# The masked score chunks of block two's window attention: a matmul with a constant, or memsets on VectorE

## The chip, the cores and the metric

One Trainium2 chip, one NeuronCore of it. The metric is the device time of the whole program in microseconds (us). Engines are called PE (TensorE's matmuls), PEld (its weight loads, which overlap the matmuls), DVE (VectorE), ACT (ScalarE), POOL (GpSimd) and SP (SyncE, which issues the DMAs). Each engine works its own instructions in order; between engines, and between dependent instructions of one engine, there are only semaphores.

## The reference, cut to what matters

Two transformer blocks over 512 tokens of width 1024, all in fp32. The change touches only the attention of the second one. Tokens lie in chunks of 64; a query sees the keys of its own chunk, whole, and of the two chunks before it:

```
qc = q.reshape(B, nc, CHUNK, ATT_KV_HEADS, ATT_GROUP, HEAD_DIM)      # CHUNK = 64, 2 kv heads, 8 heads in a group
kb = concatenate([kc[:, j:j + nc] for j in range(WINDOW_CHUNKS + 1)], axis=2)   # 3 chunks of keys
s = einsum('bnqhgd,bnkhd->bhgnqk', qc, kb) * HEAD_DIM ** -0.5
s = where(key_chunk >= 0, s, -1e30)
m = maximum(max(s), sink)
p = exp(s - m)
denom = sum(p) + exp(sink - m)
o = einsum('bhgnqk,bnkhd->bnqhgd', p / denom, vb)
```

## The kernel before, in words

Precision is kept by splitting operands into two float32r parts (`_hi`, `_lo`). A projection's weights come by DMA into `stage`, ACT rounds them to `w_hi`, DVE subtracts to get `w_lo`, and PE makes three products of each piece (hi with hi, hi with lo, lo with hi).

The window attention is a software pipeline of 32 pieces in 35 steps (`WIN_STEPS`, a lag of 3). A piece is one block of 128 queries (`b = p // 8`) and two heads that share a bank of PSUM, one in each half of 256 columns. For `b > 0` a head has 256 keys, two blocks of 128, of which each half of the query block masks one chunk: queries 64 to 127 don't see the first 64 keys, and queries 0 to 63 don't see the last 64. For `b = 0` there is only the query block's own 128 keys, and only the second of these masks. The order is written out by hand and every engine's loop runs over the same `p`:

- PE, step p (L2315 to L2361): waits until ACT has read the scores of piece p-2 (`ps_s` has two buffers); the mask product (L2324), which writes the constant -1e30 or 0 over the outer chunks by a product of the identity with `window_r`; four score products (L2332, L2334), which add to it; then for piece q = p-3 the transposes of the divided weights (L2348), 5 or 6 products of 512 columns of the next projection (`stream`, L1956), and the products with the values into `ps_o` (L2358). The last ones wait for ACT's copy of the transposed weights (`win_pt_made`), and in every second step also for `a_gated`.
- DVE, iteration p (L1742 to L1787): in every second one two gate products that read `ps_o` (L1753, 64 partitions each, they set `a_gated`); the row maximum of the scores (L1762); its minimum with the sink (L1765); the sink's difference (L1768); for piece p-1 the denominator (L1776), its reciprocal (L1777) and the division of the second head's weights (L1779); and, in some iterations, a bank of the streamed projection (L1698), its gate (L1705) or half a `w_lo` (L1177).
- ACT, iteration p (L1029 to L1067): the copy of piece p-3's transposed weights (L1036, L1038 for `b = 0`), which waits for the transposes; the two exponentials of piece p (L1049), which wait for DVE's L1765; the sink's exponential (L1055); the division of the first head's weights of piece p-1 (L1061); and in some iterations a tanh (L1010) or half a `w_hi` (L662).

`link` gives a DVE instruction an increment of DVE's own semaphore and `after` waits for it: DVE's instructions do not see each other's results otherwise. Behind the attention PE goes on with the projections of `u2` (L2362), in the same order.

Of the kernel before, what the change touches and what calls it, by code (L numbers as in the profile page):

```python
# [33 lines left out]
P = 128  # L34
# [6 lines left out]
NEG = -1e30  # L41
# [12 lines left out]
CHUNK = 64  # L54
# [52 lines left out]
def window_head(i, e):  # L107

    return 4 * (i // 2) + i % 2 + 2 * e
# [81 lines left out]
def build(nc, A):  # L191
    with ExitStack() as ctx:
# [6 lines left out]
        def keep(name, shape, dt=F32):  # L199
            return ctx.enter_context(nc.sbuf_tensor(name, shape, dt))  # L200
# [13 lines left out]
        ident_r = keep("ident_r", [P, P], F32R)  # L214
        causal_r = keep("causal_r", [P, P], F32R)
        window_r = keep("window_r", [P, 2, 2 * P], F32R)
# [66 lines left out]
        ps_s = ctx.enter_context(nc.psum_tensor("ps_s", [P, 2, S], F32))  # L283
# [866 lines left out]
        def _(dve):  # L1150
            V = nc.vector
            chain = [0]

            def link(ins):

                chain[0] += 1
                ins.then_inc(dve_chain, 1)
                return chain[0]

            def after(n):  # L1160
                dve.wait_ge(dve_chain, n)
# [261 lines left out]
            for p in range(MLA_STEPS + 3):  # L1423
                if p < NP:
                    n = P * (p % 4 + 1)
                    b = p % 4
# [5 lines left out]
                if 1 <= p <= NP:  # L1432
                    q = p - 1
                    n = P * (q % 4 + 1)
                    b = q % 4
# [12 lines left out]
                for u, m in MLA_STREAM.banks.get(p, ()):  # L1448
                    n = 2 * (u - U0["dk"]) + m
# [36 lines left out]
            for p in range(DIFF_STEPS + 1):  # L1486
# [7 lines left out]
                if p < NP:  # L1494
                    n = P * (p % 4 + 1)
                    for e in range(2):
                        b = 2 * (p % 4) + e
# [5 lines left out]
                if 1 <= p <= NP:  # L1503

                    q = p - 1
                    n = P * (q % 4 + 1)
                    b, c = q % 4, q % 8
# [7 lines left out]
                    if b == 3:  # L1515
                        c = 4 * (q // 4 % 2)
# [185 lines left out]
            def z_bank(m, n):  # L1702

                dve.wait_ge(z_tanh, n + 1)
                V.scalar_tensor_tensor(out=gu[:, n, :], in0=tmp[:, m, :], scalar=1.0, in1=gu[:, n, :], op0=ALU.add,  # L1705
                                       op1=ALU.mult).then_inc(z_gated, 1)
# [35 lines left out]
            for p in range(WIN_STEPS + 2):  # L1742
                if p > LAG and (p - LAG) % 2 == 0 and p - LAG <= NP:

                    pair = (p - LAG) // 2 - 1
                    b, c0 = pair // 4, 2 * (pair % 4)
                    dve.wait_ge(win_pv_done, 2 * pair + 2)
                    if pair == 0:
                        dve.wait_ge(za_made, KD)
                    for odd in range(2):  # L1750
                        rr = slice(odd * AD, odd * AD + AD)
                        g = gz[rr, c0:c0 + 2, b * P:b * P + P]
                        V.tensor_tensor(g, ps_o[rr, 256 * odd:256 * odd + 256].rearrange("p (c n) -> p c n", c=2), g,  # L1753
                                        ALU.mult).then_inc(a_gated, 1)
                if p < NP:
                    b, i = p // 8, p % 8
                    h = window_head(i, 0)
                    j = 16 * (b % 2) + h
                    j0 = 0 if b else P
                    dve.wait_ge(win_s_full, p + 1)  # L1760
                    mx = nmax[:, 2 * (p % 4):2 * (p % 4) + 2]
                    after(link(V.tensor_reduce(mx, ps_s[:, p % 2, :].rearrange("p (e n) -> p e n", e=2)[:, :, j0:256],  # L1762
                                               AX.X, ALU.max, negate=True)))

                    V.tensor_tensor(nm2[:, j:j + 3:2], mx, nsinkb[:, h:h + 3:2], ALU.min).then_inc(win_max_made, 1)  # L1765
                    c = 2 * (p % 4)
                    dve.wait_ge(win_max_made, p + 1)
                    V.tensor_tensor(dsink[:, c:c + 2], sinkb[:, h:h + 3:2], nm2[:, j:j + 3:2], ALU.add  # L1768
                                    ).then_inc(sink_diff, 1)
                if 1 <= p <= NP:  # L1770
                    q = p - 1
                    b, i = q // 8, q % 8
                    j0, c = 0 if b else P, 2 * (q % 4)
                    j = 16 * (b % 2) + window_head(i, 0)
                    dve.wait_ge(sink_exp, q + 1)
                    after(link(V.tensor_tensor(den2[:, c:c + 2], rs2[:, j:j + 3:2], esink[:, c:c + 2], ALU.add)))  # L1776
                    V.reciprocal(rden2[:, c:c + 2], den2[:, c:c + 2]).then_inc(rden_made, 1)  # L1777
                    dve.wait_ge(rden_made, q + 1)
                    V.tensor_scalar(prob2[:, q % 4, 256 + j0:512], prob2[:, q % 4, 256 + j0:512], rden2[:, c + 1:c + 2],  # L1779
                                    None, ALU.mult).then_inc(win_p_ready, 1)  # L1780
                for u, m in WIN_STREAM.banks.get(p - 1, ()):
                    z_bank(m, 2 * (u - U0["zs"]) + m)
                for u, m in WIN_STREAM.banks.get(p, ()):
                    normed(gu[:, 2 * (u - U0["zs"]) + m, :], u, m)
                for h in range(2):
                    for u in WIN_STREAM.started(p - 3 - h):
                        lo_half(u + 1, h)  # L1787

            for i in range(4):
# [5 lines left out]
                for m in range(2):  # L1795
                    c = 2 * i + m
# [8 lines left out]
            for i in range(4):  # L1805
                u = U0["vs"] + i
                lo(u + 1)
                for t in range(TT if i % 2 else 0):
                    n = 4 * (i // 2) + t
# [29 lines left out]
            for i in range(4):  # L1839
                u = U0["att"] + i  # L1840
                lo(u + 1)
                for m in range(2):
                    c = 2 * i + m
# [19 lines left out]
            for i in range(4):  # L1863
                u = U0["sgo"] + i
                lo(u + 1)
                for m in range(2):
                    c = 2 * i + m
# [46 lines left out]
        def _(pe):  # L1914
            T = nc.tensor
# [195 lines left out]
            for p in range(MLA_STEPS):  # L2111
                if p < NP:
                    h, t = p // 4, p % 4
                    n = P * (t + 1)
# [39 lines left out]
            for p in range(DIFF_STEPS):  # L2154
                if p < NP:
                    h, t = p // 4, p % 4
                    n = P * (t + 1)
                    for e in range(2):
# [5 lines left out]
                        for k in (kd_hi, kd_lo):  # L2164
                            T.matmul(ps_s[:, e, 0:n], qd[:, 2 * h + e, t * P:(t + 1) * P], k[:, 2 * h + e, 0:n],  # L2165
                                     start=(k is kd_hi), stop=False)
# [148 lines left out]
            for p in range(WIN_STEPS):  # L2315
                if p < NP:
                    b, i = p // 8, p % 8
                    if p >= 2:
                        pe.wait_ge(win_exp_made, 2 * (p - 1))
                    j0 = 0 if b else P  # L2320
                    k0 = (b - 1) * P if b else 0

                    ends = slice(0, 4, 3) if b else slice(3, 4)
                    T.matmul(ps_s[:, p % 2, :].rearrange("p (e c n) -> p e c n", e=2, c=4)[:, :, ends, :],  # L2324
                             ident_r[:, :], window_r[:, :, :].rearrange("p e (c n) -> p e c n", c=4)[:, :, ends, :],
                             start=True, stop=False, skip_group_check=True)


                    for e in range(2):
                        h = window_head(i, e)  # L2330
                        out = ps_s[:, p % 2, e * 256 + j0:e * 256 + 256]
                        T.matmul(out, q_split[:, h, b * P:(b + 1) * P], k_hi[:, i // 4, k0:(b + 1) * P],  # L2332
                                 start=False, stop=False, skip_group_check=True)
                        ins = T.matmul(out, q_split[:, h, b * P:(b + 1) * P], k_lo[:, i // 4, k0:(b + 1) * P],  # L2334
                                       start=False, stop=(e == 1), skip_group_check=True)
                    ins.then_inc(win_s_full, 1)
                q = p - LAG
                if 0 <= q < NP:
                    if q == 0:
                        pe.wait_ge(wg_made, 1)  # L2340
                    pe.wait_ge(win_p_ready_act, q + 1)
                    pe.wait_ge(win_p_ready, q + 1)
                    if q >= 1:
                        pe.wait_ge(win_pt_made, q)
                    for e in range(2):
                        for kb in range(0 if q // 8 else 1, 2):
                            c = (2 * e + kb) * P
                            ins = T.transpose(ps_t[:, c:c + P], prob2[:, q % 4, c:c + P], ident[:, :])  # L2348
                    ins.then_inc(win_t_full, 1)
                stream(WIN_STREAM, p, lambda u: acts_x)  # L2350
                if 0 <= q < NP:
                    b, i = q // 8, q % 8
                    pe.wait_ge(win_pt_made, q + 1)
                    if q % 2 == 0 and q:
                        pe.wait_ge(a_gated, q)
                    weights = pt2[:, q % 2, :].rearrange("p (e c n) -> p e c n", e=2, c=2)
                    for kb in range(0 if b else 1, 2):
                        ins = T.matmul(ps_o[:, 256 * (q % 2):256 * (q % 2) + 256].rearrange("p (e n) -> p e n", e=2),  # L2358
                                       v2[:, b - 1 + kb, i // 4, :], weights[:, :, kb, :],
                                       start=(kb == (0 if b else 1)), stop=(kb == 1))  # L2360
                    ins.then_inc(win_pv_done, 1)  # L2361
# [11 lines left out]
            for g in range(8):  # L2373
                if g >= 4:
                    pe.wait_ge(sg_lo_made, g - 3)
                for b in range(TT):
                    ins = T.matmul(side_bank(g)[:, b * P:(b + 1) * P], vs[:, b, g * P:(g + 1) * P], wg_t[:, g, :],
                                   start=True, stop=True)
# [59 lines left out]
```

## Time and profile before

| | us |
|---|---|
| median of 3 runs | 1287.36 |
| lowest, highest | 1286.83, 1287.45 |
| the profiled execution | 1287.28 |
| its span, first to last instruction | 1285.6 |
| PE, DVE, ACT busy | 1267.0, 726.6, 549.8 |

The span is the part of the execution that the trace covers; 1.68 us lie around it. In the rows below, times are from the span's start, durations are those of one instruction unless a row says otherwise, and "idle before" is time in which the engine had nothing to do, with the instruction that ended it. The window attention runs from 865 to 967 us of the span. The granted TensorE clock is full in all of it.

### The profile page before, as it was taken

The page shows a single profiled execution, that of the slowest core. Times are in us where ns is not written, and L with a number is a line of the kernel's source. Part 1 is how long each engine was busy: PE and PEld are TensorE (multiplying, and loading weights), DVE is VectorE, ACT ScalarE, POOL GpSimd, SP SyncE. Part 2 cuts the span into 40 slices and gives each one's busy share as a digit, 9 for nine tenths or more (in the row PEclk, how much of TensorE's full clock was granted, in tenths as well). Part 3 has the DMA queues.
Part 4 walks back from the last instruction along what each step waited for, and adds up shares of the span by engine and source line. Part 5 has one row for each costly group of instructions (what it writes and reads, how often), then busy time and mean ns, then how long its engine had stood idle before and what let it go on. Part 6 is the DMA issues. An engine that isn't in the chain of part 4 may idle for free.

```text
span 1285.6 us, 15728 instructions
## 1 busy us (share of the span) xinstructions
PE 1267.0 (99%) x6068; PEld 1054.5 (82%) x6068; DVE 726.6 (57%) x1192; ACT 549.8 (43%) x961; POOL 54.9 (4%) x97
## 2 busy tenths in 40 slices
PE   8999999999999999999999999999999999999997
PEld 6877878888888888888888888888888888888886
DVE  6776667654554444444433239858875436436554
ACT  5546655652334343434323234337773343223233
POOL 0001331220000000000000000000000000000000
PEclk9999999999999999999999999999999999999999
DMA  6332323122432333333322423331104322332221
GB/s 198 70 98 67 82 75 91 51 75 90 164 126 71 98 98 98 98 98 104 108 82 82 131 66 115 99 98 34 57 10 147 108 91 97 98 98 96 85 98 66
DMA packets 106363, 119.52 MB, mean 93 GB/s; under 512 B 13815, under 2 KB 88637, under 8 KB 106301
## 3 DMA queue, kind: packets, MB, share of 16 engines
q1 hardware_dynamic: 106160, 118.64, 29.3%
q8 instruction: 41, 0.67, 0.2%
q14 instruction: 22, 0.17, 0.0%
q10 hardware_dynamic: 140, 0.04, 0.0%
HBM read 113.42 MB, written 2.10 MB: 90 GB/s over the span
## 4 chain that ended last, share of the span: by engine, by line
PE 90%; DVE 4%; ACT 3%; POOL 2%; issue 1%; DMA 0%; SPq 0%; ACTq 0%; DVEq 0%
PE ps_mm L1956 56%; PE ps_mm L1991 22%; PE ps_o L2358 2%; PE ps_s L2120 1%; PE ps_o L2143 1%; PE ps_t L2348 1%; DVE w_lo L1168 1%; PE ps_mm L1962 1%; PE ps_mm L2051 1%; PE ps_s L2165 1%; ACT w_hi L642 1%; PE ps_o L2192 1%; PE ps_s L2334 0%; PE ps_s L2332 0%; POOL tmp L603 0%
## 5 line engine op out<-in xcount | busy, mean ns | idle before, releaser
L1956 PE MATMUL ps_mm<-act_hi,w_hi 128*128 128x512 f32 x944 | 372.8, 395 | 1.6 <-DVE w_lo L1168 1.6
L1956 PE MATMUL ps_mm<-act_lo,w_hi 128*128 128x512 f32 x944 | 370.2, 392 | 0.0
L1956 PE MATMUL ps_mm<-act_hi,w_lo 128*128 128x512 f32 x944 | 370.1, 392 | 0.0
L1168 DVE TENSOR_TENSOR w_lo<-stage,w_hi 128x2048 fp32r<-128x2048 f32 (+3 forms) x77 | 157.7, 2048 | 164.7 <-ACT w_hi L642 164.5
L1956 PEld LDWEIGHTS ps_mm<-act_hi,w_hi 128*128 128x128 f32 x944 | 177.4, 188 | 37.6 <-DVE w_lo L1168 3.3
L1956 PEld LDWEIGHTS ps_mm<-act_hi,w_lo 128*128 128x128 f32 x944 | 177.4, 188 | 35.7
L1956 PEld LDWEIGHTS ps_mm<-act_lo,w_hi 128*128 128x128 f32 x944 | 177.5, 188 | 34.4
L642 ACT ACTIVATE w_hi<-stage 128x2048 fp32r<-128x2048 f32 (+3 forms) x78 | 133.1, 1707 | 166.4 <-PE ps_mm L1991 118.9
L1572 DVE TENSOR_TENSOR w_lo<-stage,w_hi 128x2048 fp32r<-128x2048 f32 x23 | 52.7, 2293 | 56.3 <-ACT w_hi L917 56.2
L1991 PE MATMUL ps_mm<-w_hi,h_hi 128*128 128x512 f32 x176 | 68.8, 391 | 0.0
L1991 PE MATMUL ps_mm<-w_hi,act_hi 128*128 128x512 f32 x176 | 68.6, 390 | 0.0
L1991 PE MATMUL ps_mm<-w_lo,h_hi 128*128 128x512 f32 x176 | 68.5, 389 | 0.0
L1991 PE MATMUL ps_mm<-w_lo,act_hi 128*128 128x512 f32 x176 | 68.5, 389 | 0.0
L1991 PE MATMUL ps_mm<-w_hi,h_lo 128*128 128x512 f32 x176 | 68.5, 389 | 0.0
L1991 PE MATMUL ps_mm<-w_hi,act_lo 128*128 128x512 f32 x176 | 68.5, 389 | 0.0
L955 ACT ACTIVATE h_hi<-sl 128x512 f32 x22 | 13.9, 632 | 94.6 <-DVE sl L1618 94.6
L1956 PE MATMUL ps_mm<-at_hi,w_lo 128*128 128x512 f32 x128 | 49.8, 389 | 0.0
L1956 PE MATMUL ps_mm<-at_hi,w_hi 128*128 128x512 f32 x128 | 49.8, 389 | 0.0
L1956 PE MATMUL ps_mm<-at_lo,w_hi 128*128 128x512 f32 x128 | 49.8, 389 | 0.0
L917 ACT ACTIVATE w_hi<-stage 128x2048 fp32r<-128x2048 f32 x23 | 43.9, 1909 | 3.6 <-PE ps_mm L1991 3.4
L1991 PEld LDWEIGHTS ps_mm<-w_lo,act_hi 128*128 128x128 f32 x176 | 33.0, 188 | 6.9
L1991 PEld LDWEIGHTS ps_mm<-w_hi,h_hi 128*128 128x128 f32 x176 | 33.0, 188 | 6.8
(397 smaller groups left out, 2005.4 us busy)
## 6 DMA issues: line engine op xcount, KB each, us to landing
stage<-in_w_in SPq DMA_DIRECT2D x44, 1024.0 KB, 5.3
stage<-in_w_ffn_gate SPq DMA_DIRECT2D x11, 1024.0 KB, 5.3
stage<-in_w_ffn_up SPq DMA_DIRECT2D x11, 1024.0 KB, 5.3
stage<-in_w_ffn_down SPq DMA_DIRECT2D x10, 1024.0 KB, 5.0
stage<-in_w_out SPq DMA_DIRECT2D x4, 1024.0 KB, 5.3
stage<-in_w_att_out SPq DMA_DIRECT2D x4, 1024.0 KB, 5.0
stage<-in_w_sg_out SPq DMA_DIRECT2D x4, 1024.0 KB, 5.1
stage<-in_w_o SPq DMA_DIRECT2D x4, 1024.0 KB, 5.0
```

Source lines behind the costliest of these rows:

```text
L642: nc.scalar.activation(w_hi[:, s, 0:k * w], stage[:, s, 0:k * w], ACT.Copy).then_inc(w_hi_made, 1)
L917: nc.scalar.activation(w_hi[:, s, 0:k * w], stage[:, s, 0:k * w], ACT.Copy).then_inc(w_hi_made, 1)
L955: nc.scalar.activation(h_hi[:, bass.ds(j * 2 + m, 1), :], sl[:, m:m + 1, :], ACT.Copy).then_inc(h_hi_made, 1)
L1168: V.tensor_tensor(w_lo[:, s, 0:k * w], stage[:, s, 0:k * w], w_hi[:, s, 0:k * w].bitcast(F32), ALU.subtract).then_inc(w_lo_made, 1)
L1572: V.tensor_tensor(w_lo[:, s, 0:k * w], stage[:, s, 0:k * w], w_hi[:, s, 0:k * w].bitcast(F32), ALU.subtract).then_inc(w_lo_made, 1)
L1956: ins = T.matmul(ps_mm[:, 2 * bank_slot + m, :], wt[:, kk, m * P:(m + 1) * P], acts[ap][:, kk, :], start=(r == 0), stop=(r == per - 1), sk ...
L1962: ins = T.matmul(ps_mm[:, 2 * bank_slot + m, tt * w:(tt + 1) * w], acts[ap][:, kk, t * P:(t + 1) * P], wt[:, kk, :], start=(r2 == 0), stop ...
L1991: ins = T.matmul(ps_mm[:, (2 * (g % 2) + t) % 4, :], acts[ap][:, k0 + kk, t * P:(t + 1) * P], slot((w_hi, w_lo)[wp], u % 2, k, w)[:, kk, : ...
L2051: ins = T.matmul(ps_mm[:, t, :], acts_x[ap][:, kk, t * P:(t + 1) * P], slot((w_hi, w_lo)[wp], 0, 4, 512)[:, kk, :], start=(kk == 0 and n = ...
L2120: T.matmul(sb_[:, 0:n], qm[0:MQ, h, t * P:(t + 1) * P], km[0:MQ, h, 0:n], start=True, stop=False)
L2143: ins = T.matmul(ps_o[:, t * P:(t + 1) * P], vm[:, j, hh], pt[:, q % 2, j * P:(j + 1) * P], start=(j == 0), stop=(j == t))
L2358: ins = T.matmul(ps_o[:, 256 * (q % 2):256 * (q % 2) + 256].rearrange("p (e n) -> p e n", e=2), v2[:, b - 1 + kb, i // 4, :], weights[:, : ...
```

## The change

PE no longer makes the mask product; its score products start the accumulation themselves, and the two heads of a piece are two groups. DVE, in iteration p and after its wait for the scores, writes -1e30 over the masked chunks of both heads: one memset of 64 partitions by 2 x 64 elements in block 0 and two in blocks 1 to 3. It then waits for the last of them before it takes the maximum.

```diff
@@ DVE, iteration p
                     dve.wait_ge(win_s_full, p + 1)
                     mx = nmax[:, 2 * (p % 4):2 * (p % 4) + 2]
+                    sc = ps_s[:, p % 2, :].rearrange("p (e n) -> p e n", e=2)
+                    outside = link(V.memset(sc[0:CHUNK, :, 2 * P - CHUNK:2 * P], NEG))
+                    if b:
+                        outside = link(V.memset(sc[CHUNK:P, :, 0:CHUNK], NEG))
+                    after(outside)
                     after(link(V.tensor_reduce(mx, ps_s[:, p % 2, :].rearrange("p (e n) -> p e n", e=2)[:, :, j0:256],
                                                AX.X, ALU.max, negate=True)))
@@ PE, step p
-                    ends = slice(0, 4, 3) if b else slice(3, 4)
-                    T.matmul(ps_s[:, p % 2, :].rearrange("p (e c n) -> p e c n", e=2, c=4)[:, :, ends, :],
-                             ident_r[:, :], window_r[:, :, :].rearrange("p e (c n) -> p e c n", c=4)[:, :, ends, :],
-                             start=True, stop=False, skip_group_check=True)
                     for e in range(2):
                         h = window_head(i, e)
                         out = ps_s[:, p % 2, e * 256 + j0:e * 256 + 256]
                         T.matmul(out, q_split[:, h, b * P:(b + 1) * P], k_hi[:, i // 4, k0:(b + 1) * P],
-                                 start=False, stop=False, skip_group_check=True)
+                                 start=True, stop=False)
                         ins = T.matmul(out, q_split[:, h, b * P:(b + 1) * P], k_lo[:, i // 4, k0:(b + 1) * P],
-                                       start=False, stop=(e == 1), skip_group_check=True)
+                                       start=False, stop=True)
                     ins.then_inc(win_s_full, 1)
```

## Rows read from the trace of the kernel before

**Rows 1.** The page's busy times, and its chain that ended last by engine
```profile
PE 1267.0 (99%) x6068; PEld 1054.5 (82%) x6068; DVE 726.6 (57%) x1192; ACT 549.8 (43%) x961; POOL 54.9 (4%) x97
PE 90%; DVE 4%; ACT 3%; POOL 2%; issue 1%; DMA 0%; SPq 0%; ACTq 0%; DVEq 0%
```
**Rows 2.** Windows: from:to, length, then busy us of PE, PEld, DVE, ACT
```profile
911.00:934.00 23.00, 23.00 (x136) 20.51 (x135) 19.12 (x56) 17.75 (x55) 0.00 (x0) 1.00 0.15 47
```
**Rows 3.** Timeline of the weight loads: start, us; blocks 1 to 3, then block 0
```profile
914.52 0.19 PEld L2332 LDWEIGHTS ps_s<-k_hi,q_split 128*128 128x128 f32 x1
914.64 0.19 PEld L2334 LDWEIGHTS ps_s<-k_lo,q_split 128*128 128x128 f32 x1
...
876.32 0.19 PEld L2332 LDWEIGHTS ps_s<-k_hi,q_split 128*128 128x128 f32 x1
876.43 0.19 PEld L2334 LDWEIGHTS ps_s<-k_lo,q_split 128*128 128x128 f32 x1
```
**Rows 4.** Timeline of DVE around its only memset
```profile
865.70 0.68 DVE L1733 COPY wg_t<-ps_o 128x512 f32<-128x512 f32 x1
866.55 0.48 DVE L1737 MEMSET wg_t<- 64x512 f32 x1 [0.17 <-DVE wg_t L1733]
867.06 0.18 DVE L1741 TENSOR_SCALAR small<-small 128x16 f32<-128x16 f32 x1
```
**Rows 5.** Timeline of DVE, one iteration
```profile
915.31 0.69 DVE L1762 TENSOR_REDUCE small<-ps_s 128x2 f32<-128x512 f32 x1 [1.00 <-PE ps_s L2334]
916.04 0.16 DVE L1765 TENSOR_TENSOR small<-small 128x2 f32<-128x2 f32 x1
916.23 0.16 DVE L1768 TENSOR_TENSOR small<-small 128x2 f32<-128x2 f32 x1
916.31 0.15 DVE L1776 TENSOR_TENSOR small<-small 128x2 f32<-128x2 f32 x1
```
**Rows 6.** The chain of the stretch: start, us; the two gates of one iteration
```profile
886.51 0.42 DVE gz L1753
886.96 0.43 DVE gz L1753
```
**Rows 7.** Groups by line and shape, 860 to 975 us: count, busy, mean ns
```profile
L1762 DVE TENSOR_REDUCE small<-ps_s 128x2 f32<-128x512 f32 x24 | 16.6, 691 | 5.4 <-PE ps_s L2334 5.0
L1762 DVE TENSOR_REDUCE small<-ps_s 128x2 f32<-128x256 f32 x8 | 3.4, 423 | 1.0 <-PE ps_s L2334 0.8
L1779 DVE TENSOR_SCALAR prob<-prob,small 128x128 f32<-128x128 f32 x8 | 2.3, 287 | 0.3
```
**Rows 8.** DVE's waits from 867 to 959.5 us: total, times, longest
```profile
DVE small L1762 <- PE ps_s L2334: 5.8, 10, 1.0
DVE gz L1753 <- PE ps_o L2358: 5.0, 9, 0.9
```
**Rows 9.** The weight loads' waits from 867 to 967.5 us
```profile
PEld ps_o L2358 <- ACT pt L1038: 2.1, 3, 1.1
PEld ps_o L2358 <- ACT pt L1036: 1.0, 3, 0.4
```
**Rows 10.** Timeline of ACT and PEld behind the maximum of [rows 5]
```profile
919.17 0.58 ACT L1036 ACTIVATE pt<-ps_t 128x512 f32<-128x512 f32 x1
919.80 0.39 PEld L2358 LDWEIGHTS ps_o<-pt,v 128*128 128x128 f32 x2
```
**Rows 11.** Timeline, last pieces of the attention: DVE, ACT and PEld
```profile
957.32 0.69 DVE L1762 TENSOR_REDUCE small<-ps_s 128x2 f32<-128x512 f32 x1
960.24 0.58 ACT L1036 ACTIVATE pt<-ps_t 128x512 f32<-128x512 f32 x1
960.86 0.73 PEld L2358 LDWEIGHTS ps_o<-pt,v 128*128 128x128 f32 x4 [0.21 <-ACT pt L1036]
```
**Rows 12.** The chain from 957 us on: start, us, what
```profile
961.09 0.91 PE ps_o L2358 x4
...
967.14 7.98 PE ps_mm L1956 x35
```

## The prediction

> **What bounds the kernel now.** I read the page first, then the stretch of the attention by windows, then single engines in it by timeline and waits. The page says that PE is busy 99% of the span and holds 90% of the chain that ended last [rows 1], so a matmul that goes is worth its time wherever PE waits for nobody. But that is a mean over the program. In the middle of the attention's 102 us DVE is busy 19.12 of 23 us and ACT 17.75, while PE is busy all 23 [rows 2]: DVE has the least room of the three after PE. The change takes work from PE and gives it to DVE in just this stretch, so the question is how much room DVE has. Its waits for PE, up to the last pieces, are 5.8 us before the maximum and 5.0 before the gates, in 19 places: 10.8 us in all [rows 8].
>
> A second view matters as much: what joins the engines. PE's value products of one step wait for ACT's copy, the copy stands in ACT's queue behind the exponentials of the piece before, and these wait for DVE's maximum. In one case the maximum starts at 915.31 [rows 5], ACT does two exponentials, a division, a tanh and half a `w_hi`, the copy starts at 919.17 without idle time, and PE's next value weights load at 919.80, 0.05 us after the copy's end at 919.75 [rows 10]. There PE is exactly on time: any later maximum delays it. Already now the weight loads wait 3.1 us in all for these copies [rows 9].
>
> **What goes.** 32 mask products. What one costs is not its record's length, since matmuls overlap, but how long it holds the array: the load of the next but one weights starts when the matmul before it starts to stream. For the mask product this is from 914.52 to 914.64, 0.12 us, in blocks 1 to 3, and from 876.32 to 876.43, 0.11 us, in block 0 [rows 3]. 24 x 0.12 + 8 x 0.11 = 3.8 us. `start` and `stop` flags moving to the score products cost nothing that a row could show, I take 0; the wait for the buffer of scores moves to the first score product and stays what it was. No DMA, no queue of SP or POOL is touched.
>
> **What comes.** 8 memsets in block 0 and 48 in blocks 1 to 3, each of 128 elements in each of 64 partitions, into PSUM. No DVE instruction of the trace writes PSUM, so this is bounded. The nearest row is DVE's one memset, 64 x 512 into SBUF [rows 4]. It lasts 0.485 us, but starts 0.17 us behind the copy's end, where a dependent DVE instruction otherwise starts 0.04 us behind (915.31 + 0.69 = 916.00, and 916.04 [rows 5]). So its record leaves out 0.13 us at its front, and it holds the queue for 0.615 us. DVE takes (691 - 423) / 256 = 1.05 ns for one more element [rows 7]; 384 fewer elements take 0.40 us off, and 0.215 us are left for one memset here. Behind each comes a gap: 0.03 us to an independent instruction that doesn't overlap (867.06 less 867.03 [rows 4]), 0.035 to the maximum, which waits for it. In blocks 1 to 3 that is 2 x 0.215 + 0.03 + 0.035 = 0.495 us an iteration, in block 0 0.215 + 0.035 = 0.25. In all 24 x 0.495 + 8 x 0.25 = 13.9 us of new work in DVE's queue.
>
> From below, a quarter of the 0.485 is 0.12 us a memset, which makes 24 x 0.305 + 8 x 0.155 = 8.6 us. From above, an ordinary operation of 128 elements lasts 287 ns [rows 7], which makes 24 x 0.64 + 8 x 0.32 = 17.9 us. I take 0.215, which is nearest to the one memset that there is.
>
> Whether two memsets overlap is part of the price. Two short operations on all partitions start 0.08 us apart though each lasts 0.16 [rows 5], while the two gates, one on the lower and one on the upper 64 partitions, start 0.45 us apart, the whole length of the first (0.42) and a gap [rows 6]. The memsets are such a pair, so I let them stand one behind the other. The Trainium skill ("VectorE: DVE Perf Modes", Two Vector instructions with no wait between them) says the same: an instruction whose output starts in another quadrant than the last output into that memory starts only when all earlier ones have finished. By the rule that rows of equal partitions would suggest, the second memset would start 0.08 us early or more, 24 x 0.08 = 1.9 us less in all, and the forecast would be 1289.1; the pair of gates decides for the first.
>
> The same page (The TRN2 errata) puts a VectorE operation without PSUM source at 58 cycles and one for each element at 0.96 GHz. By that a memset here would be 0.19 us, an estimate, the new work 12.7 us and the time about 1289.8. No run here shows it.
>
> **The sum.** DVE's loads against PE's, blocks 1 to 3: the new 0.495 us an iteration stand against 10.8 us of waits over 32 iterations, 0.34 each, and the shorter step of PE takes 0.12 of these away. So DVE runs out of room and sets the pace. At the far end it can be read what this does to PE. The last maximum starts at 957.32; its exponentials, a division and a tanh lead without idle time to the copy at 960.24, and PE's value weights wait for that copy until 960.86 [rows 11], the products start at 961.09, and from there PE goes on to 967.14, where the next projection begins [rows 12]. So the attention ends 9.8 us behind the last maximum, now and after, and what counts is by how much that maximum slips: new work less the waits that it fills. If all are filled: 13.9 - 10.8 = +3.1 us. Not all can be: in the first iterations ACT, not DVE, sets the pace, and of the waits that lie there I leave 0.5 us unfilled. That gives +3.6 us. The 3.8 us that PE saves are in this already; they come back as waits of 3.8 + 3.6 = 7.4 us at the value products, on top of 3.1.
>
> As a second bookkeeping I stepped the three queues through the 35 steps, each operation starting at the later of its queue and its semaphores, durations from the rows of their groups. For the kernel before it ends at 967.3 us where the trace has 967.14. For the changed one it ends 3.3 us later, 3.9 where a memset also never overlaps what stands in front of it, and it puts the largest new waits (0.5 to 1.4 us) where a tanh, half a `w_hi` or half a `w_lo` falls in, as at 919.8. Both ways agree; I take +3.6.
>
> Behind 967.14 PE streams `u2`'s weights at 7.98 / 35 = 0.23 us a product [rows 12]; 48 of them, 11 us, cover DVE's next `w_lo`, so the shift goes through to the end whole. 1287.28 + 3.6 = 1290.9; the profiled execution is 0.08 below the median, so 1291.0.
>
> **The rivals.**
> DVE hides it (faster). If memsets into PSUM cost next to nothing, or overlapped the maximum's start, DVE would still wait for PE and PE would keep its 3.8 us: 1283.6. For it speaks PE's 99%; against it that at places like 919.80 there is no slack [rows 10], so that PE, its step 0.12 us shorter, only arrives earlier there and waits. Stepped with memsets at nothing the gain is only 1.5 us.
> Gain and loss cancel. With 0.12 to 0.18 us a memset, new work of 8.6 to 12 us is about what the waits hold. Stepped, it comes to +0.7 at the one end and +2.5 at the other, about 1288.8. For it: the record of the memset, taken at its word, is only 0.95 ns an element in all.
> Dear memsets. At 0.29 us the new work is 17.9 us and the last maximum slips by 17.9 - 10.8 = 7.1: 1294.4. For it: DVE has never written PSUM here, and its other operations of 128 elements last that long. It decides from 0.25 us a memset (stepped +4.5 to +5.4).
>
> **How the numbers follow.** The forecast, +2.5 to +5.4 us, 0.48; cancelled, 0.31; dear, 0.13; hidden, 0.08. The likeliest gives 1291.0, its own range is 1289.8 to 1292.7. The range for 8 times in 10 reaches over the cancelled case and half the dear one: 1286.5 to 1294.3. A measurement of this kernel tells 0.2%, 2.6 us, from no change. Faster by that needs nearly all of the hidden case: 0.06. Slower is the forecast and the dear case: 0.60. The rest, 0.34, is within.
>
> **What would show it.** In the profile after: memsets in pairs, a pair with its gaps 0.45 to 0.53 us from the scores' wait to the maximum; DVE's waits for PE's scores and gates in the stretch down from 10.8 to below 3 us; PE's waits for ACT's copies up from 3 to about 10 us, and PE's first product of the next projection near 970.7 instead of 967.14; some waits of PE for DVE's gates, which there are none of now. The mask's reasoning is wrong if the score products move apart by less than 0.12 us where PE doesn't wait. The forecast is wrong if DVE keeps over 5 us of its waits, since then it had more room or less work than I took; and the step from the last maximum to the end is wrong if that distance is no longer 9.8 us.

## The result, and the profile after

The changed kernel takes 1291.22 us (median of 8 runs, 1291.08 to 1292.85) against 1287.34 of the kernel before: ratio 1.0032, 95% interval 1.0023 to 1.0041, so 3.0 to 5.3 us slower. The profiled execution took 1291.23 us with a span of 1289.5, 3.9 us more than before's span.

The page's busy times and its chain by engine, of the changed kernel, answer to [rows 1]:

```profile
PE 1265.0 (98%) x6036; PEld 1049.8 (81%) x6036; DVE 735.3 (57%) x1248; ACT 549.3 (43%) x961; POOL 54.9 (4%) x97
PE 85%; DVE 8%; ACT 3%; POOL 2%; issue 2%; ACTq 0%; POOLq 0%; DVEq 0%
```

PE is busy 2.0 us less, the time is 3.9 us more, and DVE's share of the chain has doubled. The timeline and the waits below say why: work left PE and came back as waiting. The timeline of DVE shows the new instructions between the gates and the maximum (first an iteration of block 0, then one of blocks 1 to 3, then one without gates). In the kernel before, the maximum followed the gates at once; the last two lines are of that kernel:

```profile
883.27 0.17 DVE L1765 MEMSET ps_s<- 64x128 f32 x1
883.47 0.42 DVE L1769 TENSOR_REDUCE small<-ps_s 128x2 f32<-128x256 f32 x1
...
901.17 0.87 DVE L1753 TENSOR_TENSOR gz<-ps_o,gz 64x256 f32<-64x256 f32 x2
902.13 0.17 DVE L1765 MEMSET ps_s<- 64x128 f32 x1
902.39 0.17 DVE L1767 MEMSET ps_s<- 64x128 f32 x1
902.59 0.69 DVE L1769 TENSOR_REDUCE small<-ps_s 128x2 f32<-128x512 f32 x1
...
903.99 0.35 DVE L1786 TENSOR_SCALAR prob<-prob,small 128x256 f32<-128x256 f32 x1
904.43 0.17 DVE L1765 MEMSET ps_s<- 64x128 f32 x1
...
899.09 0.87 DVE L1753 TENSOR_TENSOR gz<-ps_o,gz 64x256 f32<-64x256 f32 x2
899.99 0.69 DVE L1762 TENSOR_REDUCE small<-ps_s 128x2 f32<-128x512 f32 x1
```

From the first memset to the maximum are 0.20 us in block 0 and 0.46 in blocks 1 to 3, and in blocks 1 to 3 the first memset starts 0.09 us behind the end of what stands in front of it (902.04, 904.34). In block 0, where the memset before it wrote the same 64 partitions, it starts 0.02 us behind (an operation that ends at 883.25). DVE's waits from 866.6 us to its last maximum, answering to [rows 8], and what the weight loads and the matmuls of PE wait for, answering to [rows 9]:

```profile
DVE gz L1753 <- PE ps_o L2359: 0.7, 2, 0.4
DVE ps_s L1765 <- PE ps_s L2335: 0.4, 2, 0.3
...
PEld ps_o L2359 <- ACT pt L1036: 6.7, 8, 1.4
PEld ps_o L2359 <- ACT pt L1038: 4.1, 3, 2.0
...
PE ps_o L2359 <- DVE gz L1753: 0.8, 2, 0.5
```

DVE has almost no wait for PE left, 0.7 + 0.4 = 1.1 us against 10.8. PE's weight loads wait 10.8 us for ACT's copies, against 3.1, and PE now waits for DVE's gates too. But ACT isn't what is late: its exponentials wait 24.9 us for DVE's minimum, where in the kernel before they waited 5.3. What ACT mostly waited for then were PE's transposes. ACT's waits, before (865 to 967 us) and after (865 to 971 us):

```profile
ACT pt L1036 <- PE ps_t L2348: 17.8, 18, 1.9
ACT prob L1049 <- DVE small L1765: 5.3, 14, 0.8
...
ACT prob L1049 <- DVE small L1772: 24.9, 25, 2.2
ACT pt L1036 <- PE ps_t L2349: 4.4, 5, 1.9
```

The last maximum on DVE's timeline, and the chain at the end of the attention, answer to [rows 11, 12]:

```profile
961.27 0.69 DVE L1769 TENSOR_REDUCE small<-ps_s 128x2 f32<-128x512 f32 x1
...
964.82 1.13 PE ps_o L2359 x4
...
971.09 14.10 PE ps_mm L1963 x62
```

The distance from the last maximum to the next projection, as the chain puts its start, is 971.09 - 961.27 = 9.82 us, as before to the hundredth.

**A sharper measure.** What lies in front of the attention varies between executions, though no code differs there: its first product started at 865.09 us of the span before and at 864.66 after, and anywhere up to 867.1 in the runs below. So beside the medians I give the attention's own length, from its first product to the first product of `u2`'s projection: 102.05 us before, 106.43 after, +4.38. It is of one profiled execution each. Nothing else in the program moves: the profiled time less the attention's start in the span and its length, which leaves what lies behind the attention and around the span, is 320.13 to 320.17 us in all fourteen profiles of this document. So the time changes only by when the attention begins and how long it is, and a median holds both. The runs below were made in three groups, each beside runs of the kernel before, which took 1287.62 us (the first four), 1288.51 (the next four) and 1288.57 (the last four); so across groups ratios and lengths are compared, not medians.

### The profile page after: what moved, and what is told of

The parts are those of the page before. It is cut to its first block, busy times and chain, and to the rows that moved or that the text cites. A ratio compares the mean times of both kernels' runs of the same rounds, so it can differ in the third digit from the quotient of the medians.

```text
span 1289.5 us, 15720 instructions
## 1 busy us (share of the span) xinstructions
PE 1265.0 (98%) x6036; PEld 1049.8 (81%) x6036; DVE 735.3 (57%) x1248; ACT 549.3 (43%) x961; POOL 54.9 (4%) x97
## 4 chain that ended last, share of the span: by engine, by line
PE 85%; DVE 8%; ACT 3%; POOL 2%; issue 2%; ACTq 0%; POOLq 0%; DVEq 0%
PE ps_mm L1963 54%; PE ps_mm L1998 22%; DVE small L1769 1%; DVE w_lo L1177 1%; PE ps_s L2127 1%; PE ps_o L2150 1%; DVE w_lo L1168 1%; PE ps_mm L1969 1%; PE ps_mm L2058 1%; PE ps_o L2359 1%; PE ps_s L2172 1%; DVE gz L1753 1%; ACT w_hi L642 1%; PE ps_o L2199 1%; POOL tmp L603 0%
## 5 line engine op out<-in xcount | busy, mean ns | idle before, releaser
L955 ACT ACTIVATE h_hi<-sl 128x512 f32 x22 | 13.9, 632 | 94.6 <-DVE sl L1618 94.6
L1049 ACT ACTIVATE prob<-ps_s,small 128x256 f32<-128x256 f32 (+1 forms) x64 | 28.0, 443 | 25.1 <-DVE small L1772 24.9
L1998 PEld LDWEIGHTS ps_mm<-w_hi,act_hi 128*128 128x128 f32 x176 | 33.0, 188 | 6.8
```

The costliest lines, as they stand in the source:

```text
L955: nc.scalar.activation(h_hi[:, bass.ds(j * 2 + m, 1), :], sl[:, m:m + 1, :], ACT.Copy).then_inc(h_hi_made, 1)
L1049: nc.scalar.activation(prob2[:, p % 4, e * 256 + j0:e * 256 + 256], ps_s[:, p % 2, e * 256 + j0:e * 256 + 256], ACT.Exp, bias=nm2[:, j:j + ...
L1998: ins = T.matmul(ps_mm[:, (2 * (g % 2) + t) % 4, :], acts[ap][:, k0 + kk, t * P:(t + 1) * P], slot((w_hi, w_lo)[wp], u % 2, k, w)[:, kk, : ...
```

## The experiments

| kernel | median us | ratio to before, 95% interval | attention us | DVE's waits | PEld's waits |
|---|---|---|---|---|---|
| before | 1287.34 | | 102.05 | 10.8 | 3.6 |
| changed | 1291.22 | 1.0032 (1.0023 to 1.0041) | 106.43 | 1.1 | 12.8 |
| both | 1293.24 | 1.0043 (1.0028 to 1.0057) | 107.43 | 2.5 | 9.9 |
| neither | 1285.46 | 0.9983 (0.9973 to 0.9992) | 99.94 | 8.8 | 5.3 |
| doubled | 1303.07 | 1.0114 (1.0097 to 1.0131) | 117.89 | 0.2 | 26.4 |
| memsets late | 1290.26 | 1.0017 (1.0008 to 1.0027) | 105.03 | 1.8 | 11.3 |
| block 0 only | 1289.41 | 1.0006 (0.9996 to 1.0015) | 102.77 | 9.8 | 5.2 |
| same half | 1290.39 | 1.0015 (1.0005 to 1.0024) | 103.95 | 2.8 | 10.2 |
| sink on ACT | 1293.35 | 1.0036 (1.0024 to 1.0047) | 106.44 | 5.3 | 12.6 |
| work on POOL | 1290.00 | 1.0013 (1.0003 to 1.0023) | 103.98 | 8.3 | 10.3 |
| changed, ACT's order | 1292.22 | 1.0025 (1.0015 to 1.0036) | 105.27 | 0.2 | 11.8 |
| changed, both moves | 1287.77 | 0.9996 (0.9986 to 1.0005) | 101.87 | 2.4 | 8.2 |
| before, ACT's order | 1287.21 | 0.9989 (0.9980 to 0.9998) | 100.29 | 8.5 | 1.2 |
| before, both moves | 1286.86 | 0.9985 (0.9976 to 0.9994) | 100.14 | 12.7 | 1.0 |

The last two columns, in us: DVE's waits for PE's scores and value products, up to the last maximum, and all waits of the weight loads in the attention. Three of these kernels leave masking out: neither and memsets late all of it, same half that of the upper 64 queries.

**Both.** The kernel before with the memsets added:

```diff
                     dve.wait_ge(win_s_full, p + 1)
+                    sc = ps_s[:, p % 2, :].rearrange("p (e n) -> p e n", e=2)
+                    outside = link(V.memset(sc[0:CHUNK, :, 2 * P - CHUNK:2 * P], NEG))
+                    if b:
+                        outside = link(V.memset(sc[CHUNK:P, :, 0:CHUNK], NEG))
+                    after(outside)
```

> The mask product stays on PE and the memsets are made as well (they overwrite what the product wrote). Theory A, VectorE's queue sets the pace of the attention once the memsets are in it: PE's 3.8 us of mask products fall into waits that it has anyway, so the time is that of the changed kernel, 1291.2 us, within 0.6. Rival B, the two costs simply add (PE's array time counts one to one, and the memsets cost 7.7 us of their own): 1291.2 + 3.8 = 1295.0 us.

The attention is 1.0 us longer than the changed kernel's, not 3.8: the product falls mostly into waits, which go down from 12.8 to 9.9 us for the weight loads. The ratio, 0.11% above the changed kernel's, is 1.4 us, with intervals that overlap. So A, but its bound of 0.6 was too tight: a quarter of the product still shows.

**Neither.** The changed kernel without its five lines on DVE.

> Neither the mask product nor the memsets: masking is left out. Theory A: PE saves 3.8 us but is early at the places where it waits for ScalarE's copies, so only part of it is kept; my stepping of the queues gave 1.5 us: 1285.8 us. Rival B: all of the product's time is kept: 1283.6 us. Together with the changed kernel this gives the whole price of the memsets, 5.4 us by A and 7.6 by B.

Nearer to A: the attention is 2.1 us shorter than before, where A had 1.5 and B the product's whole 3.8. The other 1.7 us are in the waits of PE's weight loads, which rise from 3.6 to 5.3, those for the copies from 3.1 to 4.6. And it prices the memsets: 106.43 - 99.94 = 6.5 us, half-way between A's 5.4 and B's 7.6.

**Doubled.**

```diff
                         outside = link(V.memset(sc[CHUNK:P, :, 0:CHUNK], NEG))
+                    junk = causal_r[:, :].bitcast(F32).rearrange("p (e n) -> p e n", e=2)
+                    outside = link(V.memset(junk[0:CHUNK, :, :], NEG))
+                    if b:
+                        outside = link(V.memset(junk[CHUNK:P, :, :], NEG))
                     after(outside)
```

> As the changed kernel, but behind each memset of a piece's scores another one of the same shape, into SBUF that nothing reads, before the maximum (112 memsets in place of 56). Theory A: VectorE has no waits left that could hide them (1.1 us in the profile after), so each costs its whole length and gap: 48 x 0.26 + 8 x 0.20 = 14.1 us more, 1305.3 us. Rival C, what a memset costs is mainly the wait on it, paid once for a group: 48 x 0.13 + 8 x 0.13 = 7.3 us more at most, 1298.5 us.

The attention is 11.5 us longer than the changed kernel's. Its timeline of DVE, one iteration, shows what the second pair costs:

```profile
922.95 0.17 DVE L1765 MEMSET ps_s<- 64x128 f32 x1
923.21 0.17 DVE L1767 MEMSET ps_s<- 64x128 f32 x1
923.39 0.17 DVE L1769 MEMSET causal_r<- 64x128 f32 x1
923.64 0.17 DVE L1771 MEMSET causal_r<- 64x128 f32 x1
923.84 0.69 DVE L1773 TENSOR_REDUCE small<-ps_s 128x2 f32<-128x512 f32 x1
```

From the first memset to the maximum are 0.89 us against 0.46: 0.43 us for two. In the twelve iterations with gates it is 0.49. With 0.46 as the mean of these two, and 0.20 in block 0 (0.18 in six pieces, 0.25 in two), that is 24 x 0.46 + 8 x 0.20 = 12.6 us of work, and less the 1.1 us of waits that were left 11.5. Memsets into SBUF last 0.165 us as those into PSUM do. A's 14.1 us was too much, since these memsets cost 0.18 to 0.25 us and not 0.20 to 0.26, but C's 7.3 us is excluded: each memset costs its own length, not the group one wait.

**Memsets late.** The five lines go, and behind the division at the end of DVE's iteration stand as many memsets of that shape:

```diff
                                     None, ALU.mult).then_inc(win_p_ready, 1)
+                    junk = causal_r[:, :].bitcast(F32).rearrange("p (e n) -> p e n", e=2)
+                    last = link(V.memset(junk[0:CHUNK, :, :], NEG))
+                    if b:
+                        last = link(V.memset(junk[CHUNK:P, :, :], NEG))
+                    after(last)
```

> No mask product, and the memsets are of the same number and shape, but go into SBUF that nothing reads, and stand at the end of VectorE's iteration, behind the division, not between the scores and the maximum; masking is left out. Theory A, the load on VectorE's queue is what costs: the time is that of the changed kernel, 1291.2 us, within 0.8. Rival D, it is the longer way from the scores over the maximum to the exponentials: the time is near that of the kernel with neither, 1285.8 to 1287 us.

```profile
921.11 0.35 DVE L1781 TENSOR_SCALAR prob<-prob,small 128x256 f32<-128x256 f32 x1
921.43 0.17 DVE L1784 MEMSET causal_r<- 64x128 f32 x1
921.68 0.17 DVE L1786 MEMSET causal_r<- 64x128 f32 x1
921.88 0.69 DVE L1705 SCALAR_TENSOR_TENSOR gu<-tmp,gu 128x512 f32<-128x512 f32 x1
```

The attention takes 5.1 of the memsets' 6.5 us though none lies between scores and maximum: D is out as the main cause. The missing 1.4 us may be load as well, for here the pair costs less. From the division to the next operation are 0.77 us, against 0.26 to 0.27 without memsets, so 0.50 an iteration; in the changed kernel the pair costs 0.52 behind gates (902.59 - 902.04 = 0.55, where the maximum stood 0.03 behind the gates before) and 0.63 behind a division (904.43 + 0.46 - 903.99 = 0.90, less 0.27). No run separates that from what is left of the longer way.

**Block 0 only.** The kernel before with `if b:` in front of the mask product and the memset for `b == 0`:

```diff
+                    if not b:
+                        sc = ps_s[:, p % 2, :].rearrange("p (e n) -> p e n", e=2)
+                        after(link(V.memset(sc[0:CHUNK, :, 2 * P - CHUNK:2 * P], NEG)))
```

> The mask product stays in blocks 1 to 3, and only block 0 (8 of 32 pieces) has the memset in its place. Theory A: 8 x 0.20 = 1.6 us of new work on VectorE, which still has some 10 us of waits behind it in blocks 1 to 3, against 0.9 us less on PE: no change, 1287.4 us within 0.6; the loss sits in blocks 1 to 3. Rival: the loss is made in block 0, where the steps are shortest (2.5 us against 3.2): 1289 us or more.

+0.7 us in the attention, and an interval from -0.04% to +0.15%: the loss is made in blocks 1 to 3, which hold three quarters of the pieces, with two memsets each.

**Same half.**

```diff
-                        outside = link(V.memset(sc[CHUNK:P, :, 0:CHUNK], NEG))
+                        outside = link(V.memset(sc[0:CHUNK, :, 0:CHUNK], NEG))
```

> As the changed kernel, but the second memset of a piece writes the lower 64 partitions too (first chunk), so the masking of the upper half is left out and valid scores of the lower half are lost. If memsets on different partitions wait for each other and a memset on the same partitions as the last does not: the gap from memset to memset falls from 0.26 to 0.18 us and that in front of the first by 0.1 or more, 24 x 0.18 = 4.3 us less work at most, 1288 to 1289.5 us. If the partitions play no part: 1291.2 us.

```profile
918.13 0.87 DVE L1753 TENSOR_TENSOR gz<-ps_o,gz 64x256 f32<-64x256 f32 x2
919.02 0.17 DVE L1765 MEMSET ps_s<- 64x128 f32 x1
919.17 0.17 DVE L1767 MEMSET ps_s<- 64x128 f32 x1
919.37 0.69 DVE L1769 TENSOR_REDUCE small<-ps_s 128x2 f32<-128x512 f32 x1
```

The same number of memsets of the same size makes an attention 2.5 us shorter than the changed kernel's (106.43 - 103.95); in the ratios, 1.0015 against 1.0032, it is 2.2 us, with intervals that just overlap. The second memset starts 0.15 us behind the first, not 0.26, and overlaps it; the first starts 0.02 us behind the gates, not 0.09. From the end of the gates to the maximum are 0.37 us instead of 0.55: two thirds of the pair's length are work, the rest is that the pair changes partitions. This is what the Trainium skill states ("VectorE: DVE Perf Modes", Two Vector instructions with no wait between them): what decides is whether an output starts in the same quadrant, a group of 32 partitions, as the last output into that memory. The trace of the doubled kernel agrees too: its third memset, the first into SBUF, starts 0.18 us behind the second, but 0.25 behind it in every iteration with gates, whose last output into SBUF was in the upper 64 partitions.

**Sink on ACT.** The sink's difference leaves DVE; ACT makes `exp(sink + bias)`, one instruction a head, in place of one for both.

```diff
-                    V.tensor_tensor(dsink[:, c:c + 2], sinkb[:, h:h + 3:2], nm2[:, j:j + 3:2], ALU.add
-                                    ).then_inc(sink_diff, 1)
...
+                        ins = nc.scalar.activation(esink[:, c + e:c + e + 1], sinkb[:, h:h + 1], ACT.Exp,
+                                                   bias=nm2[:, j:j + 1])
```

> The changed kernel with the sink's difference (the instruction behind the minimum) taken off VectorE: ScalarE makes the sink's exponential with the bias, one instruction a head, 0.1 us more in its queue an iteration. In the trace the difference costs VectorE 0.19 us from the minimum to the denominator, 32 x 0.19 = 6.2 us. Theory A (VectorE's queue sets the pace): about 5 of these come back, less 0.5 to 1 for ScalarE: 1287 to 1288 us. Rival E, ScalarE's queue is as much the bound: no gain, 1291 us or more.

A miss: 106.44 us, nothing gained. DVE's waits for PE rise from 1.1 to 5.3 us, so DVE's queue did get room, and it was lost again. But my price for ACT was wrong too. The timeline of ACT:

```profile
916.57 0.47 ACT L1056 ACTIVATE small<-small 128x1 f32<-128x1 f32 x2
916.94 0.50 ACT L1064 ACTIVATE prob<-prob,small 128x256 f32<-128x256 f32 x1
```

The pair holds ACT 0.37 us where the single one held it 0.09 (917.15 to 917.24 in the kernel before), 32 x 0.28 = 9 us more in ACT's queue, not 3. So the run said that ACT's queue matters as well, and left open whether less load on DVE would help. The last four kernels go into that.

**Work on POOL.** The second head's division and the gate of the projection's banks go from DVE to GpSimd:

```diff
-                    V.tensor_scalar(prob2[:, q % 4, 256 + j0:512], prob2[:, q % 4, 256 + j0:512], rden2[:, c + 1:c + 2],
+                    G.tensor_scalar(prob2[:, q % 4, 256 + j0:512], prob2[:, q % 4, 256 + j0:512],
...
+                    linked_after(G.tensor_tensor(tmp[:, m, :], tmp[:, m, :], gu[:, n, :], ALU.mult))
+                    G.tensor_tensor(gu[:, n, :], tmp[:, m, :], gu[:, n, :], ALU.add).then_inc(z_gated, 1)
```

> The changed kernel with the second head's division and the gate of the streamed projection moved from VectorE to GpSimd, which is idle in the attention: 24 x 0.27 + 8 x 0.20 + 8 x 0.60 = 12.9 us off VectorE's queue, about what the memsets put on it. Theory A, if GpSimd disturbs nobody: the time of the kernel with neither product nor memsets, 1285.5 to 1286.5 us. Rival F, VectorE's operations take longer while GpSimd works (its division of 128 elements is 756 ns in block one's attention, where GpSimd is busy, and 287 here): no gain or a loss, 1291 to 1296 us.

Between A and F: 2.5 us of the memsets' 6.5 come back. The timelines of DVE and POOL show one thing that took from the gain:

```profile
911.29 1.25 DVE L1796 TENSOR_TENSOR small<-small 128x2 f32<-128x2 f32 x1
...
911.24 1.28 POOL L635 TENSOR_TENSOR gu<-tmp,gu 128x512 f32<-128x512 f32 x1
```

A sum of two elements, 0.155 us elsewhere, ends with POOL's operation: 1.25 us. The three small additions and minima of an iteration take 20.3 us over the 32 iterations where they take 15.4 in the changed kernel. That isn't the whole of it: DVE now waits 8.3 us for PE, so it isn't the bound alone, and the division, on the way to the transposes, takes POOL 0.93 us and more (mean 1.15) where it took DVE 0.35. How the lost 4.0 us divide between the two isn't shown.

**ACT's order, and both moves.** ACT's tanh and half `w_hi` are kept until behind the next copy; with both moves POOL also makes the sink's difference (two elements), at no cost to ACT. Each on the changed kernel and on the one before.

```diff
+                for work in later:
+                    work()
+                later = []
                 if p < NP:
                     b = p // 8
                     act.wait_ge(win_max_made, p + 1)
...
-                    z_bank(u, m)
+                    later.append(lambda u=u, m=m: z_bank(u, m))
...
-                        hi_half(u + 1, h)
+                        later.append(lambda u=u, h=h: hi_half(u + 1, h))
@@ with both moves, GpSimd
+                G.tensor_tensor(dsink[:, c:c + 2], sinkb[:, h:h + 3:2], nm2[:, j:j + 3:2], ALU.add
+                                ).then_inc(sink_diff, 1)
```

> The changed kernel with ScalarE's extra work (tanh, half a w_hi) moved from the end of its iteration to behind the next copy, in front of the exponentials, where it waits 24.9 us for VectorE's maxima. Theory A (VectorE's queue, with 1.3 us of waits left, is the bound): at most 1.3 us come back, 1290 to 1291 us. Rival G, the way from a late maximum through ScalarE's queue to the copy is the bound: the tanh and the half w_hi leave that way, 3 us or more come back, 1288 us or less.

> As the one before, and the sink's difference (two elements) goes from VectorE to GpSimd; ScalarE's sink exponential stays one instruction. VectorE loses 0.19 us an iteration, 6.1 us, at no cost on ScalarE. Theory A with the loop through ScalarE relieved: the time falls by about 5 us against the kernel before this one, 1285.5 to 1287 us. If the move of the difference to ScalarE gained nothing for another reason than ScalarE's longer queue: 1290 us or more.

> The kernel before (mask product) with ScalarE's order changed as above. Its PE waits 3.6 us at the weight loads for ScalarE's copies, all at places where a tanh or half a w_hi lies between. If these go: 1 to 3 us faster than the kernel before, 1284.5 to 1286.5 us. If the work only delays the next exponentials and by them the next copy: no change, 1287.4 us.

> The kernel before with both moves. VectorE isn't the bound there (10.8 us of waits), so the second move adds little: within 0.7 us of the kernel with the first move alone, 1284 to 1286.5 us.

On the changed kernel the order alone gives 1.2 us in the attention, within A's 1.3 and not G's 3 (the median, 1292.22 us, doesn't show it; in the profiled execution the attention began at 867.1 us). The waits of PE's products for DVE's gates rise from 0.8 to 4.0 us: what ACT's order clears, DVE's queue takes up. Taking 6.1 us off DVE's queue then gives another 3.4 us; in the ratios 1.0025 and 0.9996, 0.29% or 3.7 us, with intervals that don't overlap. So less load on DVE helps where ACT's queue isn't lengthened for it and its order is changed. That speaks for ACT's price as the reason why the sink on ACT missed; no run has the difference on POOL with ACT's old order, which would tell the price from the order. On the kernel before the order gives 1.8 us and takes the weight loads' waits from 3.6 to 1.2 us, those for the copies from 3.1 to 0.3, and the second move adds 0.15, as expected where DVE isn't the bound. The kernel before with both moves has the lowest ratio of those that mask, 0.9985 (0.9976 to 0.9994), though not clear of the order alone (0.9989). With the same two moves the changed kernel is still 1.7 us slower in the attention (101.87 against 100.14); the ratios, 0.11% apart, have intervals that overlap.

## Why the prediction was right

The time lies 0.2 us from the forecast of 1291.0 and the mechanism is the one forecast. That it is so close is partly luck: the attention grew by 4.4 us, 0.8 more than the sum's 3.6, and in the profiled execution it began 0.43 us earlier. Step by step:

- **What PE saves**, 0.12 us a product. Right: in the chain of the changed kernel's attention only the four score products are left between the value products and the transposes, 939.47 - (938.13 + 0.86) = 0.48 us = 4 x 0.12. Before it was 937.57 - (936.11 + 0.86) = 0.60, five of them (the last two lines). That saving only gives 2.1 of its 3.8 us even when nothing is added (neither), and 1.0 where the memsets are there too (both against changed).

```profile
938.13 0.86 PE ps_o L2359 x4
939.47 0.44 PE ps_t L2349 x4
...
936.11 0.86 PE ps_o L2358 x4
937.57 0.44 PE ps_t L2348 x4
```

- **What a memset costs.** I took 0.215 us and a gap of 0.03, from the one memset into SBUF. Its record is 0.165 us and the gap 0.09, which comes to 0.255 against 0.245. The sizes of two parts were off and made up for each other. That writing PSUM might be dear or cheap didn't come true either way, 0.165 us in either memory. The estimate of 0.19 us that stood beside it lies above the record and below the distance of 0.26.
- **Memsets one behind the other.** Right, and the run with the same half shows the price, 2.5 us of the loss where the prediction had 1.9 for a second memset that overlaps. What I had put only into the second bookkeeping, that the first memset doesn't overlap what stands in front of it either, belongs in the sum: 0.52 us an iteration behind gates and 0.63 behind a division, about 24 x 0.575 + 8 x 0.20 = 15.4 us of work, not 13.9.
- **The waits that are filled.** 10.8 us, of which 0.5 to stay. 1.1 are left, so 9.7 are filled. 15.4 - 9.7 would be 5.7, yet the last maximum slips 4.4 us against the attention's start. Between them may lie that 15 of the 19 waits are gone, and an operation behind a filled wait starts about 0.08 us before the end of the one in front, 1.2 us in all: worked out, not shown by a run. That was missing in my sum, and it made up for most of what the low price of the memsets left out. Of the 0.8 us that remain, 0.6 are the waits that stayed, 1.1 us and not 0.5.
- **From the last maximum to the end**, 9.8 us, one to one. Right: 9.82 us before and after, and 9.81 or 9.82 in "both", "neither", "doubled", "block 0 only" and "same half" too. It holds while DVE's and ACT's work behind the maximum stays what it is; in the other kernels it is 9.24 to 10.31.
- **PE's waits** went from 3.6 to 12.8 us where I had about 10 for the copies; for the copies alone it is 10.8. The next projection began at 971.09, I had 970.7, from a start that was 0.43 us earlier.

The rivals: that DVE hides the memsets fails on its 1.1 us of waits; that gain and loss cancel needed new work of 8.6 to 12 us and dear memsets 17.9, where it is about 15.4. The record of 0.165 us does lie within the 0.12 to 0.18 that the first of these named; what lifts the price are the gaps that the record leaves out. What I said too simply is that DVE sets the pace. It sets it through ACT's queue: DVE's load counts (late, doubled, both moves), but the sink on ACT points to ACT's queue, between the maximum and the copy, as counting too, and the order of ACT alone is worth 1.8 us in the kernel before. How the 6.5 us of the memsets divide between the two for each step of the pipeline stays open.

## What to carry to other kernels

An engine that is busy 99% of the time is not paid for every matmul that goes: read the room of the engine that gets the work, as the sum of its waits in that very stretch, and compare it with the new instructions at their start-to-start distance, gaps included. A matmul of 0.12 us can't be traded for two vector instructions of 0.26 us each in a stage where the vector engine has 0.34 us an iteration. Before moving work, look at what an engine does last in its iteration: work that nobody waits for belongs where that engine waits anyway.

## What the runs showed of the hardware that I had not expected

- A memset of 128 elements in 64 partitions lasts 0.165 us in its record into PSUM and into SBUF; start to start it is 0.14 to 0.15 us to one on the same partitions and 0.26 us to one on the other half.
- A two-element addition on DVE took 1.25 us while GpSimd worked on a 512-element sum in SBUF, and a division of 256 elements takes GpSimd 0.93 us, 1.15 in the mean, where it takes DVE 0.35.
- One activation of two elements holds ACT 0.09 us, two activations of one element with a bias 0.37.
- The time in front of the attention varies by 2.4 us between the profiled executions (864.66 to 867.10), though no code of PE, DVE or ACT differs up to there. PE's busy time in the first 100 us differs too (91.2 to 92.2). The cause is open.
